# Four-bank decay rows, closer last SSD groups, halved opening units and a per-token final norm in a two-layer hybrid decoder trunk

## The reference

```
for i in range(2):
    x = x + 0.5 * swiglu(rmsnorm(x, g), w_gate_up, w_down)       # 1024 -> 2*2816 -> 1024
    x = x + (short_conv if i == 0 else ssd)(rmsnorm(x, g))
    x = x + memory_cross_attention(rmsnorm(x, g), rmsnorm(mem, g'))   # 4 heads, 256 memory tokens
    x = x + 0.5 * swiglu(rmsnorm(x, g), w_gate_up, w_down)
return rmsnorm(x, final_gain)

# ssd, per head h and chunk: a_cum = cumsum(dt * -exp(a_log))
decay[l, s] = exp(a_cum[l] - a_cum[s]) for s <= l, else 0       # 128 x 128 per head and chunk
y = (cb * decay) @ (x * dt) + C @ state * exp(a_cum) + x * d_skip
y = y * silu(z); y = y * rsqrt(mean(y*y over a group's 256 channels) + eps) * gate_norm; y @ w_out
```

## Time and profile before

| what | value |
|---|---|
| median of 3 runs | 1339.04 us (1337.76 to 1341.26) |
| profiled execution: its own time | 1343.49 us |
| its span, first to last instruction | 1341.7 us |
| mean granted clock | 0.991 |
| busy: PE / DVE / ACT / POOL | 96% / 75% / 56% / 17% |
| DMA | 228.3 MB, mean 170 GB/s |

### The profile page before, as it was taken

One profiled execution on the slowest core, in us unless ns is written; L12 is line 12 of the kernel. 1 busy time (PEld: TensorE's weight loads), 2 busy tenths in 40 slices (PEclk: granted clock), 3 DMA queues, 4 the chain that ended last, 5 costly groups with the idle time before them and its releaser, 6 DMA issues.

```text
span 1341.7 us, 24083 instructions
## 1 busy us (share of the span) xinstructions
PE 1294.3 (96%) x8324; PEld 1169.4 (87%) x8324; DVE 1002.5 (75%) x1553; ACT 756.5 (56%) x1362; POOL 231.6 (17%) x316
## 2 busy tenths in 40 slices
PE   6999999999999999999999997999979999999996
PEld 5888889989998888888888885899979999888885
DVE  6887767687768888668887666798856767888764
ACT  6555544356556556446555554678855655655641
POOL 2333111112001111101111100024451201111111
PEclk9999999999999999999999999999999999999998
DMA  6656655545445556645556443344344543555750
GB/s 241 192 187 205 199 167 171 183 157 186 129 142 181 188 183 218 195 146 178 183 187 230 166 167 126 123 149 138 126 142 170 164 149 133 186 182 186 225 192 32
DMA packets 60120, 228.32 MB, mean 170 GB/s; under 512 B 6673, under 2 KB 7953, under 8 KB 59793
## 3 DMA queue, kind: packets, MB, share of 16 engines
q1 hardware_dynamic: 60048, 227.39, 51.8%
HBM read 226.31 MB, written 1.05 MB: 169 GB/s over the span
## 4 chain that ended last, share of the span: by engine, by line
PE 79%; DVE 10%; ACT 5%; issue 3%; POOL 2%; DMA 0%; DVEq 0%; ACTq 0%; SPq 0%; POOLq 0%
PE bank L1175 79%; DVE w_lo L673 3%; ACT w_hi L343 3%; DVE acc L676 2%; DVE decay L943 1%; DVE acc L673 1%; DVE x L673 1%; ACT sq L376 1%; ACT corr L343 1%; POOL ssq L1087 0%; DVE t L673 0%; ACT h L343 0%; POOL y L1156 0%; DMA x<-x_t 0%; POOL root_y L1138 0%
## 5 line engine op out<-in xcount | busy, mean ns | idle before, releaser
L1175 PE MATMUL bank<-h,w_hi 128*128 128x512 f32 (+1 forms) x2056 | 621.3, 365 | 15.5 <-DVE w_lo L673 10.3
L673 DVE TENSOR_TENSOR w_lo<-raw,w_hi 128x1024 fp32r<-128x1024 f32 (+1 forms) x401 | 521.6, 1304 | 54.2 <-ACT w_hi L343 52.7
L1175 PE MATMUL bank<-h,w_lo 128*128 128x256 f32 x1736 | 489.3, 282 | 0.0
L343 ACT ACTIVATE w_hi<-raw 128x1024 fp32r<-128x1024 f32 (+1 forms) x401 | 442.1, 1103 | 45.3 <-PE bank L1175 44.1
L1175 PE MATMUL bank<-a,w_hi 128*128 128x512 f32 (+1 forms) x1664 | 461.2, 348 | 0.2 <-DVE w_lo L673 0.2
L1175 PEld LDWEIGHTS bank<-h,w_hi 128*128 128x128 f32 x2056 | 367.7, 190 | 83.7 <-issue 10.2
L1175 PE MATMUL bank<-a,w_lo 128*128 128x256 f32 x1280 | 360.8, 282 | 0.0
L1175 PEld LDWEIGHTS bank<-h,w_lo 128*128 128x128 f32 x1736 | 330.4, 190 | 0.0
L1175 PEld LDWEIGHTS bank<-a,w_hi 128*128 128x128 f32 x1664 | 290.1, 191 | 42.3 <-issue 0.5
L1175 PEld LDWEIGHTS bank<-a,w_lo 128*128 128x128 f32 x1280 | 243.8, 190 | 0.0
L343 ACT ACTIVATE corr<-bank 128x256 f32<-128x256 f32 x233 | 88.5, 381 | 267.6 <-PE bank L1175 267.6
(11 more groups left out here) (177 smaller groups left out, 1115.6 us busy)
## 6 DMA issues: line engine op xcount, KB each, us to landing
raw<-w_gu SPq DMA_DIRECT2D x176, 512.0 KB, 3.6
raw<-w_down SPq DMA_DIRECT2D x64, 704.0 KB, 4.1
raw<-w_xbc SPq DMA_DIRECT2D x32, 512.0 KB, 3.5
raw<-w_conv_in SPq DMA_DIRECT2D x24, 512.0 KB, 4.1
raw<-w_q SPq DMA_DIRECT2D x16, 512.0 KB, 4.2
raw<-w_k SPq DMA_DIRECT2D x16, 512.0 KB, 4.2
raw<-w_v SPq DMA_DIRECT2D x16, 512.0 KB, 3.6
raw<-w_o SPq DMA_DIRECT2D x16, 512.0 KB, 3.7
```

The source lines that it names most:

```text
L343: return nc.scalar.activation(out, in_, ACT.Copy, scale=scale)
L673: return nc.vector.tensor_tensor(out, a, b, op)
L1175: return nc.tensor.matmul(out, lhs, rhs, start=start, stop=stop, skip_group_check=check)
```

## The change

Four independent edits.

1. **Decay rows.** Four banks (5, 6, 4, 7) instead of two; PE's pair j waits for the differences of pair j-4. ACT's exponentials come one step later (`decays_by(s - 2)`). The low part of the rows is made before ACT loads its Exp table, and DVE finishes it in the same step. The low parts of the eight `normed` blocks move from DVE to POOL.
2. **Last groups.** A table `due` gives each step of each group its t; for groups 5 to 7 it is nearer. At t = 40 PE runs six of the eight blocks of the first second-half unit ahead of group 7's transposes, and six blocks of the next two behind them.
3. **The start.** x comes in five pieces, units 0 and 1 in halves (unit 0 from ACT's DMA queue), each half split on its own; the memory input is loaded later, in four pieces; PE runs five matmuls on ones first; `norm_sums` comes behind unit 3, `norm_spread` behind unit 4; the four products of units 0 to 3 stand together.
4. **The final norm.** ACT multiplies each block of x by the gain, PE transposes it to tokens on partitions (7 of the 8 ahead of `norm_sums`), and the root is then a scalar per partition: DVE and ACT each evict two tiles of 128 x 512, and four DMAs of 256 KB go out, one of them from ACT. The spread is gone.

```diff
+        DECAY_BANKS = (5, 6, 4, 7)
+        TAIL = {"y": {7: 35}, "state": {7: 36}, "y_add": {7: 36}, "yo": {6: 34, 7: 36}, "yoff": {6: 35, 7: 37},
+                "square": {6: 36, 7: 38}, "root": {6: 36, 7: 38}, "yn": {5: 35, 6: 37, 7: 39}, "yt": {5: 35, 6: 38, 7: 40}, "a_rest": {5: 36, 6: 39, 7: 40}}
...
+                load_x(0, 1)
+                load_x(1, 2)
+                load_x(2, 4)
+                sp.dma_start(raw[:, 1, 0:HALF_W], w[1][:, 0:HALF_W]).then_inc(half_in[1], 16)
+                load_x(4, 6)
+                load_x(6, 8)
+                sp.dma_start(raw[:, 1, HALF_W:UNIT_W], w[1][:, HALF_W:UNIT_W]).then_inc(landed[1], 16)
...
@@ ACT, ssd, s == 4
+                        act.wait_ge(row_rest, 1)
+                        copy(rows[0:2 * H, :], acc[0][0:2 * H, :]).then_inc(row_lo, 1)
                         nc.scalar.activation(e_acum[:, :], d["nacum"][:, 1, :], ACT.Exp, scale=-1.0).then_inc(acum_exp, 1)
                         nc.scalar.activation(dsd[:, :], rest[:, :], ACT.Exp).then_inc(acum_exp, 1)
-                        act.wait_ge(row_rest, 1)
-                        copy(rows[0:2 * H, :], acc[0][0:2 * H, :]).then_inc(row_lo, 1)
...
-                    while lcount < decays_by(s - 1):
+                    while lcount < decays_by(s - 2):
                         decays(lcount)
...
@@ DVE, ssd
-                    if 5 < s <= 5 + KT:
-                        normed_lo(s - 6)
...
@@ POOL, ssd
+                for k in range(KT):
+                    pool.wait_ge(nhi_ready, k + 1)
+                    nc.gpsimd.tensor_tensor(a_lo[:, H_NORMED + k, :], normed[k], a_hi[:, H_NORMED + k, :].bitcast(F32), ALU.subtract).then_inc(nh_ready, 1)
...
@@ PE, decays
-                at_least(pe, diff_ready, j - 1)
+                at_least(pe, diff_ready, j - 3)
...
-                    ins = mm(bank[5 + j % 2][:, r * SEQ:r * SEQ + SEQ], ...)
+                    ins = mm(bank[DECAY_BANKS[j % 4]][:, r * SEQ:r * SEQ + SEQ], ...)
...
@@ PE, start
+            for i in range(5):
+                mm(bank[7][:, 0:SEQ], ones[:, :], ones[:, 0:1].broadcast_to((P, SEQ)), True, True)
...
+                    half_units()
+                    one_unit(2, bank[2], KT, 0, h, True, True)
+                    one_unit(3, bank[3], KT, 0, h, True, True)
+                    norm_sums(b)
+                    one_unit(4, free(name, 4), KT, 0, h, True, True)
+                    pe.wait_ge(eye_in, 16)
+                    norm_spread(b)
+                    for t in range(5, 8):
+                        one_unit(t, free(name, t), KT, 0, h, True, True)
...
@@ PE, ssd
+                    if t == SSD_UNITS:
+                        second_halves(range(1), range(KT - 2))
...
+                second_halves(range(1, 3), range(KT - 2))
+                second_halves(range(3), range(KT - 2, KT))
+                second_halves(range(3, KT), range(KT))
...
@@ end
+            for k in range(KT - 1):
+                turn_final(k)
             norm_sums(NORM_FINAL)
-            norm_spread(NORM_FINAL)
+            turn_final(KT - 1).then_inc(turned, 1)
...
-            for k in range(KT):
-                stt(a_out(k), x[:, k, :], gain(NORM_FINAL, k), bank[4][:, 0:SEQ]).then_inc(out_ready, 1)
+            for c in range(2):
+                cols = slice(c * 512, c * 512 + 512)
+                nc.vector.tensor_scalar(final[:, 0, cols], bank[FINAL_BANKS[0][c]][:, :], rms_n[:, 0:1], None, ALU.mult).then_inc(out_ready, 1)
```

More of the change, by code:

```diff
@@ L278, in trunk @@
         PAIRS = GROUPS * HPG // 2
+        DECAY_BANKS = (5, 6, 4, 7)
         def decays_by(s):
             return 0 if s < 5 else min(PAIRS, s - 4 if s < 12 else 2 * s - 15)
-        SSD_STEPS = 4 * (GROUPS + 3) + 2
         SSD_UNITS = 4 * GROUPS + KT
+        SSD_STEPS = SSD_UNITS + 2
+        TAIL = {"y": {7: 35}, "state": {7: 36}, "y_add": {7: 36}, "yo": {6: 34, 7: 36}, "yoff": {6: 35, 7: 37},
+                "square": {6: 36, 7: 38}, "root": {6: 36, 7: 38}, "yn": {5: 35, 6: 37, 7: 39}, "yt": {5: 35, 6: 38, 7: 40}, "a_rest": {5: 36, 6: 39, 7: 40}}
+        STEADY = {"cb": 4, "xt": 5, "b_nat": 5, "m0": 5, "m1": 6, "xn": 6, "y": 9, "zs": 9, "state": 10, "y_add": 10, "yo": 11,
+                  "yoff": 12, "square": 13, "root": 14, "yn": 15, "yt": 16, "a_rest": 17}
+        due = {}
+        for stage, after in STEADY.items():
+            for g in range(GROUPS):
+                due[stage, TAIL.get(stage, {}).get(g, 4 * g + after)] = g
         block = ctx.enter_context(nc.Block())
@@ L317, in load_phase @@
                 else:
-                    with sp.Fori(1, units // SLOTS) as i:
+                    with sp.Fori(3 if name == "gu0" else 1, units // SLOTS) as i:
                         for s in range(SLOTS):
@@ L441, in project_out @@
                     square(b, k)
+                    if b == NORM_FINAL:
+                        copy(mem[:, k, :], x[:, k, :], gain(b, k)).then_inc(scaled, 1)
             def conv():
@@ L576, in ssd @@
                         silu_xbc(*divmod(t - 1, 4))
-                    g = G - 2
-                    if 0 <= g < GROUPS and q == 2:
+                    if ("state", t) in due:
+                        g = due["state", t]
                         act.wait_ge(state_done, g + 1)
@@ L634, in silu_xbc, with half_split @@
                 nc.scalar.activation(out, acc[q % 2][:, :], ACT.Silu).then_inc(xbc_ready, 1)
+            nc.scalar.dma_start(raw[:, 0, 0:HALF_W], w_gu[0][0][:, 0:HALF_W]).then_inc(half_in[0], 16)
+            nc.scalar.dma_start(raw[:, 0, HALF_W:UNIT_W], w_gu[0][0][:, HALF_W:UNIT_W]).then_inc(landed[0], 16)
+            act.wait_ge(ones_set, 1)
+            copy(corr[0][:, 0:P], ones[:, :])
+            def half_split(n, part):
+                if part == 0:
+                    act.wait_ge(half_in[n], 16)
+                    copy(w_hi[n][:, 0:HALF_W], raw[:, n, 0:HALF_W]).then_inc(hi_half, 1)
+                else:
+                    act.wait_ge(landed[n], 16)
+                    copy(w_hi[n][:, HALF_W:UNIT_W], raw[:, n, HALF_W:UNIT_W]).then_inc(hi_ready, 1)
             act.wait_ge(gain_in, 16)
             for k in range(KT):
[L639 to L642 removed]
+                if k in x_in:
+                    act.wait_ge(x_in[k], 16)
                 new_h(0, k)
[L644 to L648 removed]
+                if k in (0, 1):
+                    half_split(0, k)
+                if k in (3, 5):
+                    half_split(1, (k - 3) // 2)
+            split(2)
+            for k in range(3):
+                square(0, k)
+            split(3)
+            for k in range(3, KT):
                 square(0, k)
@@ L659, in _ @@
             ffn(3)
+            act.wait_ge(rms_n_ready, SS_INDEX[NORM_FINAL] + 1)
+            act.wait_ge(turned, 1)
+            for c in range(2):
+                cols = slice(c * 512, c * 512 + 512)
+                copy(final[:, 1, cols], bank[FINAL_BANKS[1][c]][:, :], rms_n[:, 1:2]).then_inc(out_ready_act, 1)
+            act.wait_ge(out_ready_act, 2)
+            nc.scalar.dma_start(out_t[:, 1, 512:], final[:, 1, 512:]).then_inc(out_landed, 16)
         @block.vector
@@ L1408, in wide_unit, with second_halves @@
                     ins.then_inc(unit_done, 1)
+            def second_halves(ks, part):
+                for k in ks:
+                    out = bank[k] if k < 4 else free("ssd_out", k)
+                    unit(first["xbc"] + SSD_UNITS + k, half(out, k), KT, KT, a, False, True,
+                         ready=(yt_ready, 0) if k == 0 else None, check=True, part=part)
             def ssd():
@@ L1505, in ssd @@
                         ins.then_inc(xt_done, 1)
-                for k in range(KT):
-                    out = bank[k] if k < 4 else free("ssd_out", k)
-                    unit(nx + SSD_UNITS + k, half(out, k), KT, KT, a, False, True,
-                         ready=(yt_ready, 0) if k == 0 else None, check=True)
+                second_halves(range(1, 3), range(KT - 2))
+                second_halves(range(3), range(KT - 2, KT))
+                second_halves(range(3, KT), range(KT))
             pe.wait_ge(ones_set, 1)
-            pe.wait_ge(gain_in, 16)
+            for i in range(5):
+                mm(bank[7][:, 0:SEQ], ones[:, :], ones[:, 0:1].broadcast_to((P, SEQ)), True, True)
             ffn(0)
```

256 lines of the change are left out of this document (158 added, 98 removed).

## The result

The changed kernel took 1321.63 us by the median of four runs (1318.65 to 1323.59); the kernel before, beside it, 1340.15 (1337.76 to 1341.81). The ratio is 0.986, with a 95% interval from 0.984 to 0.988. In a second set of runs the medians were 1318.63 and 1339.12, 0.985 (0.983 to 0.988). So it is faster by 18.5 to 20.5 us. The time lies in the forecast range (1310 to 1323), 6 above the forecast of 1315.5.

What follows compares the result with a forecast made beforehand. PE, busy 96% of the 1341.7 us span, was taken as the bound, so edits gain only from its waits and lower clock. 13.7 + 7.0 + 0.4 + 2.4 = 23.5 gave 1320.0 profiled, median 1315.5, range 1310 to 1323.

Steps and rivals of the forecast that it cites:

- the ring: z stage: DVE and ACT take turns, 4.64 us a step; exponentials a step later cut this, part of 13.7 gained.
- at most 3.24: z stage: PE's own work in a step, from pairs of decay rows 4.64 us apart with 1.40 of waiting.
- The clock's 1.5: z stage: loss to the lower clock behind the wait of 3.73 us, expected to be regained.
- The 1.1 for the rows: z stage: PE's wait for the rows the decay differences are made from, expected to go, 1.1 us.
- DVE could become the bound: z stage rival: POOL's subtractions block DVE, whose step then exceeds PE's; 8.9 us lost, 1324.4; chance 0.10.
- That rival's second price: z stage: with half of POOL's 1.65 us holding DVE, 3.54 lost at most, giving 1319; rival's chance 0.10.
- its scaling is at 985.10 to 985.7 ... PE waits 1.3: Last SSD groups: group 5's transposes wait 1.3 us for DVE's scaling, as POOL's root for it hasn't moved.
- POOL's chain: Last SSD groups rival: POOL's work holds group 7's transposes, a wait of 5 us; gain 1, not 7; 1321.5; chance 0.12.
- The forecast's waits of 1.1 and 0.8: Last SSD groups: PE's remaining waits in us, before group 7's transposes and the fourth second half; gain taken as 7.0.
- From 1.5 lost to 1.5 gained, I take 0.4: Start: PE's early lead is spent in a new wait before unit 6, leaving 0.4 us gained.
- 1.9 and some 0.4 for the larger transfer: Final norm: time in us from the last DMA issue to the span's end, at 1339.2; gain 2.4.
- The slower rival: Whole kernel: new short waits keep PE's clock at 0.50, deciding from 24 us of work; 1340 and up; chance 0.03.

Runs made afterwards that it cites:

- the fourteen traces: One profiled execution each of the kernel before, the changed kernel and the twelve follow-up runs, whose medians were 1309.36 to 1332.71 us.
- the changed kernel's second execution: Nothing changed against the changed kernel, which was run and profiled again: median 1318.63 us, ratio 0.985 to the kernel before.

## Why the prediction was right, and where its terms were not

**z stage: mechanism right, size low by 2.7.** That the exponentials' place made the ring was shown by undoing it alone (14.0). The term that I mis-sized is the step of PE: I let "at most 3.24" stand and counted only the rows of the waits, while each also cost the run-out of PE's pipe. PE's step without waits is 3.00, so 0.24 came on top of each of some 11 waits, 2.6 in all: 13.7 + 2.6 = 16.3 against 16.4. I had named it, as the upper bound of 15.5, and not taken it; even that bound was 0.9 too low. The clock's 1.5 was right: the step behind the wait of 3.73 took 4.48 instead of 3.00. The 1.1 for the rows went too (the first pair stands 15.07 behind the root and not 16.38), but its edit was not undone by itself. That DVE could become the bound did not happen. My sign for it, splits clearly over 1.23, did come, with 1.65 in two steps, and PE still waited for nothing: DVE had the room. With the subtraction back on DVE the time was the same. That rival's second price was also mis-summed: with half of POOL's 1.65 the step is 3.53, 0.29 over 3.24, so 2.3 in eight steps and not 3.54.

**Last groups: 3.7 instead of 7.0.** The step that failed is "its scaling is at 985.10 to 985.7 ... PE waits 1.3". I took the scaling's 0.62 from a place where POOL was idle, although the same edit lets POOL's sum start at that very moment: 2.13, against 0.61 once POOL was held back. The Trainium skill, SBUF — State Buffer, "SBUF: two separate sides", says that of a GpSimd instruction and a vector instruction in a two-port performance mode, or with two SBUF inputs, whichever starts first holds the shared ports for its whole instruction and the other is blocked. POOL's row (967.46) begins just ahead of DVE's (967.54). Taken singly, the two scalings ended at 968.33 and 969.67, each 0.15 behind the end of one of POOL's two instructions (968.18 and 969.52), so the trace agrees; whether the scaling was in such a mode no run shows. I had weighed that rule for the z stage only. The other half of the failure is the clock, which I let stand at full rate behind the new waits. Together the two cost 4.6. What I feared instead, POOL's chain, gave no wait: group 7's transposes ran at 990.13. That is 22.6 behind group 5's scaling, over the 20 that I had named as the sign of this rival, but it was PE that came late. So that rival was wrong here, though with group 5's wait gone the chain was ready only 0.1 ahead of PE. The forecast's waits of 1.1 and 0.8 in front of group 7 and the fourth second half were 0 and 0.2, so 1.7 of the 4.6 came back; 0.4 of the 3.3 missed stays open.

**Start: -2.1 instead of 0.4.** The chain came out as forecast: the root ended at 25.05 (24 to 25), unit 6's low part at 31.54 (30.2 to 31.6), the wait was 3.27 (2 to 4). The step that failed is "From 1.5 lost to 1.5 gained, I take 0.4". That PE starts unit 6 later than before, by 0.64, was inside these bounds; the lower clock behind the wait was not, and cost 1.5. I had dismissed it with the wait of 1.40 of the earlier trace rows, behind which the pair took its usual 0.50. A wait of 1.40 said nothing of one of 3: in the fourteen traces the clock was at 0.50 behind each of the ten waits of 2.56 to 2.58 and each of the seven of 3.16 to 3.31 in front of unit 6. But below that the length doesn't decide. A wait of 1.88 for `h`, near 299 us and untouched by any edit, was followed by 0.50 in eleven traces and by 1.00 in three, which made that stage 0.7 shorter; here in the kernel before and in the changed kernel's second execution:

```profile
298.96 0.51 PE L1175 MATMUL bank<-h,w_hi 128*128 128x256 f32 x2 [1.88 <-DVE h L676]
299.39 0.51 PE L1263 MATMUL bank<-h,w_hi 128*128 128x256 f32 x2 [1.88 <-DVE h L744]
```

```profile
300.00:302.00 2.00, 2.00 (x11) 2.00 (x11) 1.42 (x3) 1.62 (x4) 0.00 (x0) 0.50 0.36 145
300.40:302.40 2.00, 2.00 (x19) 2.00 (x19) 1.42 (x3) 1.60 (x4) 0.00 (x0) 1.00 0.40 164
```

So the 1.86 and 2.34 behind which the clock stayed up, each seen once, don't show that such waits are free.

**End: 1.5 instead of 2.4.** The evictions took 0.7 (0.65) and SP's last issue ended at 1315.5; the forecast's 1336.9, moved by the 21.3 gained up to there, is 1315.6. What failed is "1.9 and some 0.4 for the larger transfer": behind the last issue came 3.4. A DMA of 256 KB took 2.9 to 3.1 from issue to landing, one of 128 KB 2.0. Before, the DMAs came one by one every 0.47; now four of twice the size come within 0.9 and follow each other. What holds them is open: no run varied the number, the size or the order of these DMAs.

**The sum.** The forecast missed by 2.7 low, 3.3, 2.5 and 0.9 high, 4.0 in all, and the pace of the feed-forward blocks, 3.2 in the second and again in the last, moves a single execution by as much. That may also be why the first set of runs was 3 slower than the second, but only one run of each has a trace. The slower rival named a real mechanism, the clock behind new waits, but it cost 1.5 and 3.1 us in two places, not the 24 from which it would decide.

## What to carry to other kernels

Where two engines take turns with each other's output, look first for the consumer that can be put one step later: here one number in ACT's order gave 14 us, and banks and a third engine's help gave 2.6 and nothing. When an order is drawn closer together, take each duration from the neighbours that it will have, not from those it had: what starts at that moment on POOL is part of the price. And price a new wait of PE with the clock behind it (1.5 and 3.1 us behind the two of 3.27 and 2.56 here), or cover it with the unit next in line.

## What the runs showed of the hardware that was not expected

- The same loop of matmuls, at a granted clock of 1.00 and with PE never idle, runs at 2.83 or at 2.77 us a unit, 2% apart. In the second and the last feed-forward block it keeps one pace throughout (3.2 us on 184 to 188), and another execution may have the other; the third block always took 187.9. No cause is shown.
- DVE's scaling of 128 x 256 (two instructions) took 1.65 to 2.22 when POOL ran beside it, and 0.61 and 0.62 when not; its split of 128 x 1024 up to 1.65 against 1.23.
- Waits of PE of 1.45 to 1.49, two in each of the fourteen traces, were all followed by the full granted clock, and those of 2.56, 3.27 and 3.73 by 0.50. One of 1.88 was followed by 0.50 in eleven traces and by 1.00 in three, and those in front of PE's first unit in the changed start, 0.93 to 1.79, by 0.50 in eight of twelve. Seven matmuls whose result nothing reads, put into the wait of 3.27, kept it at 1.00.
- Asking for Silu first took a table load of 1.28 off the path, and unit 6 started 0.8 earlier by it; ACT's copies and squares ran behind it without one of their own.
